# The low half of the rope keys for the second half of the queries: two products over 64 rows each, in opposite halves of TensorE's rows, in place of two products over 128 rows

## The chip, the cores and the metric

The kernel runs on one core of a Trainium2 chip. The metric is the device time of one execution in microseconds (us); a change is judged by the median of several executions.

## The reference

The reference is a decoder trunk of two layers over 256 tokens with a model width of 2048: a causal pooling layer, then a multi-head latent attention layer, each followed by a SwiGLU feed-forward part, and a final RMSNorm. What matters here is the score of each head:

```
sc = (jnp.einsum('bqhd,bkhd->bhqk', q_nope[:, s0:e], k_nope[:, :e])
      + jnp.einsum('bqhr,bkr->bhqk', q_pe[:, s0:e], k_pe[:, :e]))
sc = sc.astype(jnp.float32) * ATTN_SCALE
```

There are 16 heads. `q_nope` and `k_nope` have 128 features a head; `q_pe` has 64 rope features a head, and `k_pe`, also 64 features, is shared by all heads. The queries come in two blocks of 128: the first sees 128 keys, the second all 256. A masked softmax over the keys and the product with `v` follow.

## The kernel before, in words

Every operand of a product is split into a high and a low part, and a product is the sum high by high, high by low and low by high, each a matmul of its own into the same PSUM bank. ScalarE writes the high parts (of weights: `split`, L814) and VectorE subtracts to get the low parts (`split`, L1199). Weights arrive by DMA in chunks of up to 704 KB.

The attention works on pairs of heads, g = 0 to 7. TensorE runs nine slots in program order. Slot g (function `slot` in the TensorE block) makes queries, keys and values of pair g, and between these it does the attention of pair g - 1, so that the softmax of that pair (VectorE and ScalarE) lies beside matmuls of pair g. The order in a slot is: `query_rope_part` (12 matmuls), `scores` of the two heads hh = 0 and 1 of pair g - 1 (16 matmuls), `query_part` (24), `key_part` (24), `turn_probs` (six transposes), `value_part` (24), `head_output` (12). The last slot, g = 8, has parts of the output projection (`wo_part`) in place of the products of a pair.

`scores` writes head hh into bank SCORES + hh. Of the bank's 512 columns, columns 0 to 127 are the first query block against the first 128 keys and 384 to 511 hold the low part of that product; columns 128 to 383 are the second query block against all keys. The lines are L634, L635 and L636 for the first block, and for the second L640 to L642 (the 128 plain features) and L644 and L645 (the rope features). For the rope features `qpe_buf` holds the high part of a head's queries in one half of the 128 partitions and the low part in the other; head 1 has the halves the other way round. `kpe[:, 0]` holds the high keys in both halves, so L644 adds high by high and low by high in one matmul. `kpe[:, 1 + hh]` holds the low keys in the 64 partitions where head hh has its high queries, and zeros in the other 64. L645 multiplies all 128 rows with it: 64 rows count, 64 are multiplied by zero.

What follows the scores: the instruction of L645 raises `scores_ready`. VectorE (`row_max`, L1483 and on) waits for it, head 0 first; then come ScalarE's exponentials, VectorE's `rope_cos`, `normalise` (L1496, L1498), two splits of weights, `pair_lo` of queries and keys, `rope_lo`, and `probT_lo_half` (L1469), which raises `probT_split`. `head_output` (first matmul L671) of the same slot waits for it. In the same function, L598, L599 and L600 are `value_part`, L652 is `turn_probs`, L412 to L414 are the products of queries and keys.

The order of all queues is written out by hand; nothing else (no planner) orders the work.

Of the kernel before, what the change touches and what calls it, by code (L numbers as in the profile page):

```python
# [44 lines left out]
P = 128  # L45
SEQ = 256
# [4 lines left out]
NOPE, ROPE, V_DIM = 128, 64, 128  # L51
# [43 lines left out]
def chunk_plan():  # L95

    chunks, tiles, c, t = {}, {}, 0, 0
    for name, nc_, nt in (
        ("pool", 2 * GROUPS, DT),
        ("up0", 4 * FH, 2 * FH), ("down0", 2 * DT, DT), ("up1", 4 * FH, 2 * FH), ("down1", 2 * DT, DT),  # L100
        ("qa", 2 * LT, LT), ("kva", 2 * LT, LT), ("kpe", 2, 2),
        ("heads", 4 * HG, 8 * HG), ("wo", 2 * DT, DT),
        ("up2", 4 * FH, 2 * FH), ("down2", 2 * DT, DT), ("up3", 4 * FH, 2 * FH), ("down3", 2 * LAST_DT, LAST_DT), ("last", LAST_CHUNKS, 2),
    ):
        chunks[name], tiles[name] = c, t
        c, t = c + nc_, t + nt
    chunks["end"] = c
    return chunks, tiles


CHUNK, TILE = chunk_plan()
# [26 lines left out]
def plus(n, i, per):  # L138

    return n if i is None else i * per + n  # L140


def trunk(nc, xT, positions, consts, bands, gains, pool_w, w_kv_a, w_k_pe, w_q_a, w_kv_k, w_kv_v, w_q_nope, w_q_pe,
          w_o, w_gate, w_up, w_down, w_last, final_gain, out):
    with ExitStack() as ctx:
        def sem(name):
            return ctx.enter_context(nc.semaphore(name))
# [31 lines left out]
        def at(name, shape, dt, offset):  # L179
            return nc.alloc_sbuf_tensor_at(name, shape, dt, offset=offset)  # L180
# [21 lines left out]
        q_buf = at("q_buf", [P, 2, 2, 2 * SEQ], F32R, region_at + 8 * KB)  # L202
        v_buf = at("v_buf", [P, 2, 2, 2, 2 * V_DIM], F32R, region_at + 16 * KB)
        qpe_buf = at("qpe_buf", [P, 2, 2, SEQ], F32R, region_at + 24 * KB)
        kpe = at("kpe", [P, 3, SEQ], F32R, region_at + 28 * KB)
        heads = at("heads", [P, HG, 2, 2 * SEQ], F32R, region_at + 32 * KB)
# [24 lines left out]
        ps = ctx.enter_context(nc.psum_tensor("ps", [P, 8, 512], F32))  # L231

        SCORES, HEADS_OUT, STATS = 4, 6, 7
# [9 lines left out]
        evacuated = sem("evacuated")  # L243
# [38 lines left out]
        qpe_ready = sem("qpe_ready")  # L282
        kpe_ready = sem("kpe_ready")
# [6 lines left out]
        probT_split = sem("probT_split")  # L290
# [109 lines left out]
        def _(pe):  # L400
# [175 lines left out]
            def key_part(g, i=None):  # L576
                n, t = CHUNK["heads"] + 4 * g + 2, TILE["heads"] + 8 * g + 4
                pe.wait_ge(lo_ready, plus(made(n), i, BODY))
                for m in range(2):
                    bank_free(t + m, i, 16)  # L580
                    for kt in range(LT):
                        mm = product_one(n, m * LT + kt, (t + m) % 4, latent[:, KV, kt, :], kt == 0, kt == LT - 1)
                mm.then_inc(chunks_used, 1)
# [19 lines left out]
            def query_rope_part(g, i=None):  # L603
                n, t = CHUNK["heads"] + 4 * g, TILE["heads"] + 8 * g
                pe.wait_ge(lo_ready, plus(made(n), i, BODY))
                bank_free(t, i, 16)
                for kt in range(LT):
                    mm = product_one(n, kt, t % 4, latent[:, Q, kt, :], kt == 0, kt == LT - 1)
                mm.then_inc(chunks_used, 1)

            def query_part(g, i=None):
                n, t = CHUNK["heads"] + 4 * g + 1, TILE["heads"] + 8 * g + 2
                pe.wait_ge(lo_ready, plus(made(n), i, BODY))
                for m in range(2):
                    bank_free(t + m, i, 16)
                    for kt in range(LT):
                        mm = product_one(n, m * LT + kt, (t + m) % 4, latent[:, Q, kt, :], kt == 0, kt == LT - 1)
                mm.then_inc(chunks_used, 1)

            def scores(g, hh, i=None):  # L620

                b = g % 2
                if hh == 0:
                    pe.wait_ge(evacuated, plus(TILE["heads"] + 8 * g + 6, i, 16))
                    pe.wait_ge(qpe_ready, plus(g + 1, i, 2))
                    if g == 0:
                        pe.wait_ge(kpe_ready, 2)
                    if g >= 1:

                        pe.wait_ge(probT_split, plus(g, i, 2))  # L630
                bank = ps[:, SCORES + hh, :]
                first, k_both = slice(0, P), k_buf[:, b, hh, :].rearrange("p (o t) -> p o t", o=2)
                apart = bank.rearrange("p (c t) -> p c t", c=4)[:, 0:4:3, :]
                pe.matmul(apart, q_buf[:, b, hh, 0:P], k_both[:, :, 0:P], start=True, stop=False)  # L634
                pe.matmul(bank[:, first], q_buf[:, b, hh, SEQ:SEQ + P], k_buf[:, b, hh, 0:P], start=False, stop=False)  # L635
                pe.matmul(apart, qpe_buf[:, b, hh, 0:P], kpe[:, 0:2 + hh:1 + hh, 0:P], start=False, stop=True)  # L636
                dst, cols = bank[:, P:3 * P], slice(P, SEQ)
                q_hi, q_lo = q_buf[:, b, hh, cols], q_buf[:, b, hh, SEQ + P:]
                k_hi, k_lo = k_buf[:, b, hh, 0:SEQ], k_buf[:, b, hh, SEQ:]
                pe.matmul(dst, q_hi, k_hi, start=True, stop=False)  # L640
                pe.matmul(dst, q_hi, k_lo, start=False, stop=False)
                pe.matmul(dst, q_lo, k_hi, start=False, stop=False)  # L642
                both = qpe_buf[:, b, hh, cols]
                pe.matmul(dst, both, kpe[:, 0, :], start=False, stop=False)  # L644
                mm = pe.matmul(dst, both, kpe[:, 1 + hh, :], start=False, stop=True)  # L645
                mm.then_inc(scores_ready, 1)

            def turn_probs(g, hh, i=None):

                pe.wait_ge(prob_ready, plus(2 * (2 * g + hh + 1), i, 8))  # L650
                for c in range(3):
                    mm = pe.transpose(ps[:, SCORES + hh, c * P:(c + 1) * P], prob[:, hh, c * P:(c + 1) * P],  # L652
                                      const[:, C_IDENT:C_IDENT + P])
                mm.then_inc(probT_ready, 1)
# [21 lines left out]
            def wo_part(c, i=None, each=None):  # L676

                n, t = CHUNK["wo"] + c, TILE["wo"] + 4 * (c // BODY) + c % 4
                half = c // 4 % 2
                pe.wait_ge(lo_ready, plus(made(n), i, BODY))  # L680
                if half == 0:
                    bank_free(t, i, 4)
                for j in range(TILES):
                    kt = half * TILES + j
                    if each is not None:
                        each(kt)
                    mm = product3(n, j, t % 4, heads[:, kt // 2, kt % 2, :], kt == 0, kt == DT - 1)
                mm.then_inc(chunks_used, 1)

            def slot(g, i=None):  # L690


                own = g < HG
                if own:
                    query_rope_part(g, i)
                else:
                    wo_part(0)
                if g >= 1:
                    scores(g - 1, 0, i)
                    scores(g - 1, 1, i)  # L700
                if own:
                    query_part(g, i)
                    if g == 0:
                        pe.wait_ge(lat_ready, 2 * LT)
                    key_part(g, i)
                else:
                    wo_part(1)
                    wo_part(2)
                if g >= 1:
                    turn_probs(g - 1, 0, i)  # L710
                    turn_probs(g - 1, 1, i)
                if own:
                    value_part(g, i)
                else:
                    wo_part(3)
                if g >= 1:
                    head_output(g - 1, 0, i)
                    head_output(g - 1, 1, i)

            pe.wait_ge(lat_ready, LT)  # L720
            slot(0)
            slot(1)

            with pe.Fori(0, HG // 2 - 1) as i:
                slot(2, i)
                slot(3, i)
# [52 lines left out]
            both = LAST_CHUNKS - SPLIT_SLOTS  # L779
# [7 lines left out]
            for c in range(both, LAST_CHUNKS):  # L787
                pe.wait_ge(lo_ready, made(CHUNK["last"] + c))
                mm = last_part(c, 0)
# [1000 lines left out]
```

## Time and profile before

| | |
|---|---|
| median of 3 runs | 1781.75 us (1781.26 to 1782.9) |
| the profiled execution | 1783.35 us, its span 1781.4 us |
| TensorE (matmuls), busy | 1766.1 us, 99% of the span |
| TensorE weight loads, busy | 1562.5 us, 88% |
| TensorE's share of the chain that ended last | 97% |
| VectorE, ScalarE, GpSimd, busy | 64%, 51%, 6% |
| mean granted TensorE clock | 0.999 |
| attention slots g = 1 to 8 in the span | about 846 to 960 us |

The span is the time from the first to the last instruction; the execution's own time is a little longer. A row of the matmul engine shows how long one matmul was in the pipeline, which overlaps with the next; what a matmul costs in a stream is the distance from its start to the next start. "PEld" is the loading of a matmul's stationary operand, one for each matmul, which runs beside the matmul before.

### The profile page before, as it was taken

To read this page: it belongs to the slowest core of one execution; us is meant where nothing else is said; L and a number is where in the kernel's file an instruction comes from. 1 tells how busy PE (TensorE), PEld (TensorE's weight loads), DVE (VectorE), ACT (ScalarE), POOL (GpSimd) and SP (SyncE) were. 2 spreads that over 40 slices of the span, in tenths; PEclk is the share of its full clock that TensorE was granted. 3 is DMA by queue.
4 is the path that set the end of the run, shared out by engine and by line. 5 is a ranking of instruction groups with operands and counts; after the bars stand their busy time and mean duration, and the time that the engine had idled before them with its cause. 6 is when DMAs were issued, how large, how long until landed. Compare 5 with 4: busy or idle time off the path is not lost.

```text
span 1781.4 us, 29177 instructions
## 1 busy us (share of the span) xinstructions
PE 1766.1 (99%) x10376; PEld 1562.5 (88%) x10376; DVE 1137.8 (64%) x1456; ACT 915.5 (51%) x1176; POOL 113.2 (6%) x129
## 2 busy tenths in 40 slices
PE   9999999999999999999999999999999999999998
PEld 5888888888888888888999888888888888888886
DVE  4866666556666666668997776666655566666553
ACT  5766664334444444455775456666533344445433
POOL 2200000000000001123112420000000000000000
PEclk9999999999999999999999999999999999999999
DMA  6555557545555566544444555555665455556641
GB/s 250 198 190 189 190 189 238 193 158 173 188 188 188 188 224 199 174 152 138 142 154 154 189 189 188 189 188 188 221 204 177 156 189 188 190 190 223 225 147 71
DMA packets 85008, 328.26 MB, mean 184 GB/s; under 512 B 9568, under 2 KB 10336, under 8 KB 84832
## 3 DMA queue, kind: packets, MB, share of 16 engines
q1 hardware_dynamic: 84816, 326.57, 54.6%
q10 hardware_dynamic: 144, 1.05, 0.1%
q8 instruction: 30, 0.49, 0.1%
q14 instruction: 18, 0.15, 0.0%
HBM read 325.48 MB, written 2.10 MB: 184 GB/s over the span
## 4 chain that ended last, share of the span: by engine, by line
PE 97%; DVE 2%; ACT 0%; DMA 0%; issue 0%; POOL 0%; SPq 0%; ACTq 0%; POOLq 0%; DVEq 0%
PE ps L404 57%; PE ps L405 30%; PE ps L475 2%; PE ps L412 1%; PE ps L413 1%; PE ps L414 1%; PE ps L765 1%; PE ps L763 1%; PE ps L764 1%; DMA raw<-pool_w 0%; DVE w_lo L1199 0%; PE ps L598 0%; PE ps L599 0%; PE ps L600 0%; POOL square_sum L1672 0%
## 5 line engine op out<-in xcount | busy, mean ns | idle before, releaser
L1199 DVE TENSOR_TENSOR w_lo<-raw,w_hi 128x1024 fp32r<-128x1024 f32 (+2 forms) x564 | 737.5, 1309 | 421.0 <-ACT w_hi L814 418.7
L404 PE MATMUL ps<-xg,w_hi 128*128 128x512 f32 x2880 | 999.5, 390 | 0.5 <-issue 0.5
L814 ACT ACTIVATE w_hi<-raw 128x1024 fp32r<-128x1024 f32 (+2 forms) x565 | 632.0, 1120 | 552.5 <-PE ps L405 538.2
L405 PE MATMUL ps<-xg,w_lo 128*128 128x256 f32 x2880 | 812.1, 282 | 0.0
L404 PEld LDWEIGHTS ps<-xg,w_hi 128*128 128x128 f32 x2880 | 540.4, 188 | 113.8 <-issue 0.6
L405 PEld LDWEIGHTS ps<-xg,w_lo 128*128 128x128 f32 x2880 | 544.3, 189 | 0.1
L404 PE MATMUL ps<-act,w_hi 128*128 128x512 f32 x1320 | 458.0, 390 | 0.0
L405 PE MATMUL ps<-act,w_lo 128*128 128x256 f32 x1320 | 372.2, 282 | 0.0
L404 PEld LDWEIGHTS ps<-act,w_hi 128*128 128x128 f32 x1320 | 247.7, 188 | 51.9
L405 PEld LDWEIGHTS ps<-act,w_lo 128*128 128x128 f32 x1320 | 249.5, 189 | 0.0
L1279 DVE TENSOR_TENSOR sums<-ps,cross 128x512 f32<-128x512 f32 x88 | 60.9, 692 | 95.5 <-ACT cross L891 95.5
L891 ACT ACTIVATE cross<-ps 128x512 f32<-128x512 f32 x88 | 52.6, 598 | 120.6 <-PE ps L405 120.5
L404 PE MATMUL ps<-heads,w_hi 128*128 128x512 f32 x256 | 89.1, 391 | 0.0
L1630 POOL TENSOR_TENSOR square<-x 128x256 f32 (+1 forms) x32 | 33.2, 1039 | 765.2 <-DVE x L1300 765.2
L405 PE MATMUL ps<-heads,w_lo 128*128 128x256 f32 x256 | 72.2, 282 | 0.0
L1299 DVE TENSOR_TENSOR x<-ps,x 128x256 f32 (+1 forms) x76 | 32.1, 422 | 54.9 <-PE ps L405 54.9
L1283 DVE TENSOR_TENSOR sums<-sums,rstd 128x512 f32<-128x512 f32 x88 | 60.9, 692 | 3.0
L894 ACT ACTIVATE gate_act<-sums 128x256 f32<-128x256 f32 x88 | 36.8, 418 | 46.0 <-DVE sums L1283 45.8
L826 ACT ACTIVATE xg<-x,gain 128x256 fp32r<-128x256 f32 (+1 forms) x48 | 23.4, 508 | 66.5 <-DVE x L1300 62.1
L404 PEld LDWEIGHTS ps<-heads,w_hi 128*128 128x128 f32 x256 | 48.1, 188 | 9.9
L405 PEld LDWEIGHTS ps<-heads,w_lo 128*128 128x128 f32 x256 | 48.4, 189 | 0.0
L412 PE MATMUL ps<-latent,w_hi 128*128 128x256 f32 x160 | 45.2, 283 | 2.5 <-DVE gate_act L1456 2.3
(196 smaller groups left out, 1227.7 us busy)
## 6 DMA issues: line engine op xcount, KB each, us to landing
raw<-w_gate SPq DMA_DIRECT2D x176, 512.0 KB, 3.2
raw<-w_up SPq DMA_DIRECT2D x176, 512.0 KB, 3.2
raw<-w_down SPq DMA_DIRECT2D x120, 704.0 KB, 4.1
raw<-w_o SPq DMA_DIRECT2D x32, 512.0 KB, 3.2
raw<-w_last SPq DMA_DIRECT2D x11, 512.0 KB, 3.2
raw<-pool_w SPq DMA_DIRECT2D x8, 512.0 KB, 12.0
raw<-w_q_a SPq DMA_DIRECT2D x8, 512.0 KB, 3.3
raw<-w_kv_a SPq DMA_DIRECT2D x8, 512.0 KB, 3.2
```

Source lines behind the costliest of these rows:

```text
L404: pe.matmul(ps[:, bank, :], w_hi[:, s, j * P:(j + 1) * P], moving, start=start, stop=False)
L405: return pe.matmul(ps[:, bank, 0:SEQ], w_lo[:, s, j * P:(j + 1) * P], moving[:, 0:SEQ], start=False, stop=stop)
L412: pe.matmul(dst, w_hi[:, s, j * P:(j + 1) * P], moving[:, 0:SEQ], start=start, stop=False)
L475: mm = pe.matmul(ps[:, 4 + 2 * (g % 2) + s, :], x_pool[:, GT * g + kt, s * P:(s + 1) * P], raw[:, c, j * GT * P:(j + 1) * GT * P], start=( ...
L814: nc.scalar.activation(dst, src, ACT.Copy).then_inc(hi_ready, 1)
L891: nc.scalar.activation(cross[:, :, :], ps[:, bank:bank + 2, SEQ:], ACT.Copy).then_inc(cross_ready, 1)
L894: nc.scalar.activation(gate_act[:, :], sums[:, 0, :], ACT.Silu).then_inc(gate_ready, 1)
L1199: nc.vector.tensor_tensor(lo, src, hi.bitcast(F32), ALU.subtract).then_inc(lo_ready, 1)
L1279: nc.vector.tensor_tensor(sums[:, :, :], ps[:, bank:bank + 2, 0:SEQ], cross[:, :, :], ALU.add).then_inc(evacuated, 2)
L1283: nc.vector.tensor_tensor(sums[:, :, :], sums[:, :, :], r, ALU.mult).then_inc(sums_ready, 1)
L1299: step(nc.vector.tensor_tensor(xd, ps[:, b, 0:SEQ], xd, ALU.add))
L1630: step(nc.gpsimd.tensor_tensor(square[:, :], src, src, ALU.mult))
```

## The change

A new function `rope_low` issues the two matmuls of L645, of both heads, ahead of `scores`. Each is restricted to the 64 partitions that count: head 0 has partitions 0 to 63, head 1 has 64 to 127, and they go to banks SCORES and SCORES + 1. They now open the accumulation of their bank (`start=True`), and L634 and L640 no longer do. The waits that stood at the head of `scores` move into `rope_low`, in the same place of the stream. `scores` then has seven matmuls a head, and the one of L644 raises `scores_ready`. The number of matmuls stays at 16 a pair of heads.

```diff
+            def rope_low(g, i=None):
+                b = g % 2
+                pe.wait_ge(evacuated, plus(TILE["heads"] + 8 * g + 6, i, 16))
+                pe.wait_ge(qpe_ready, plus(g + 1, i, 2))
+                if g == 0:
+                    pe.wait_ge(kpe_ready, 2)
+                if g >= 1:
+                    pe.wait_ge(probT_split, plus(g, i, 2))
+                for hh in range(2):
+                    rows = slice(ROPE * hh, ROPE * hh + ROPE)
+                    pe.matmul(ps[:, SCORES + hh, P:3 * P], qpe_buf[rows, b, hh, P:SEQ], kpe[rows, 1 + hh, :],
+                              start=True, stop=False)
...
             def scores(g, hh, i=None):
                 b = g % 2
-                if hh == 0:
-                    pe.wait_ge(evacuated, plus(TILE["heads"] + 8 * g + 6, i, 16))
-                    pe.wait_ge(qpe_ready, plus(g + 1, i, 2))
-                    if g == 0:
-                        pe.wait_ge(kpe_ready, 2)
-                    if g >= 1:
-                        pe.wait_ge(probT_split, plus(g, i, 2))
...
-                pe.matmul(apart, q_buf[:, b, hh, 0:P], k_both[:, :, 0:P], start=True, stop=False)
+                pe.matmul(apart, q_buf[:, b, hh, 0:P], k_both[:, :, 0:P], start=False, stop=False)
...
-                pe.matmul(dst, q_hi, k_hi, start=True, stop=False)
+                pe.matmul(dst, q_hi, k_hi, start=False, stop=False)
...
-                both = qpe_buf[:, b, hh, cols]
-                pe.matmul(dst, both, kpe[:, 0, :], start=False, stop=False)
-                mm = pe.matmul(dst, both, kpe[:, 1 + hh, :], start=False, stop=True)
+                mm = pe.matmul(dst, qpe_buf[:, b, hh, cols], kpe[:, 0, :], start=False, stop=True)
                 mm.then_inc(scores_ready, 1)
...
                 if g >= 1:
+                    rope_low(g - 1, i)
                     scores(g - 1, 0, i)
                     scores(g - 1, 1, i)
```

## Rows read from the trace of the kernel before

**Rows 1.** The page: busy us, share of the span and instructions of each engine.

```profile
PE 1766.1 (99%) x10376; PEld 1562.5 (88%) x10376; DVE 1137.8 (64%) x1456; ACT 915.5 (51%) x1176; POOL 113.2 (6%) x129
```

**Rows 2.** Busy time by window, slot 3: window, length, PE, PEld, DVE, ACT, POOL.

```profile
873.90:887.80 13.90, 13.90 (x119) 13.90 (x120) 12.97 (x33) 10.34 (x22) 1.60 (x2) 1.00 0.43 135
```

**Rows 3.** Waits between 859 and 943.3: us in total, times, longest.

```profile
DVE prob L1483 <- PE ps L645: 2.8, 6, 0.7
...
PE ps L671 <- DVE probT L1469: 0.4, 1, 0.4
```

**Rows 4.** Timeline of slots 2, 3 and 7: VectorE's chain and TensorE's start on `head_output`.

```profile
863.73 0.29 DVE L1483 TENSOR_TENSOR prob<-ps,const 128x128 f32<-128x128 f32 x1 [0.67 <-PE ps L645]
...
872.85 0.95 DVE L1469 TENSOR_TENSOR probT<-ps,probT 128x768 fp32r<-128x768 f32 x1
...
873.46 0.28 PE L600 MATMUL ps<-w_hi,latent 128*128 128x256 f32 x1
873.90 0.36 PE L671 MATMUL ps<-probT,v_buf 128*128 128x256 f32 x1 [0.17 <-issue]
...
886.63 0.95 DVE L1469 TENSOR_TENSOR probT<-ps,probT 128x768 fp32r<-128x768 f32 x1
...
887.63 0.28 PE L600 MATMUL ps<-w_hi,latent 128*128 128x256 f32 x1
887.75 0.29 PE L671 MATMUL ps<-probT,v_buf 128*128 128x256 f32 x1
...
942.53 0.95 DVE L1469 TENSOR_TENSOR probT<-ps,probT 128x768 fp32r<-128x768 f32 x1
...
942.95 0.27 PE L600 MATMUL ps<-w_hi,latent 128*128 128x256 f32 x1
943.58 0.36 PE L671 MATMUL ps<-probT,v_buf 128*128 128x256 f32 x1 [0.35 <-issue]
```

**Rows 5.** Timeline of TensorE in slot 3, head 0 of the scores.

```profile
876.75 0.28 PE L634 MATMUL ps<-k_buf,q_buf 128*128 128x256 f32 x1
...
876.93 0.33 PE L636 MATMUL ps<-kpe,qpe_buf 128*128 128x256 f32 x1
877.10 0.28 PE L640 MATMUL ps<-k_buf,q_buf 128*128 128x256 f32 x1
...
877.58 0.28 PE L645 MATMUL ps<-kpe,qpe_buf 128*128 128x256 f32 x1
877.70 0.28 PE L634 MATMUL ps<-k_buf,q_buf 128*128 128x256 f32 x1
```

**Rows 6.** Timeline of TensorE in `head_output` of slot 2: two matmuls of 128 columns.

```profile
874.39 0.28 PE L672 MATMUL ps<-probT,v_buf 128*128 128x128 f32 x1
874.50 0.27 PE L673 MATMUL ps<-probT,v_buf 128*128 128x128 f32 x1
```

**Rows 7.** Line L645: duration ns least/median/most, first and last start.

```profile
L645 PEld LDWEIGHTS ps<-kpe,qpe_buf x16: 187/188/192, 847.5 to 949.5; 128*128 128x128 f32 x16
```

**Rows 8.** Timeline of TensorE in slot 2, into and out of the six transposes.

```profile
869.96 0.28 PE L414 MATMUL ps<-latent,w_lo 128*128 128x256 f32 x1
870.08 0.82 PE L652 MATMUL ps<-const,prob 128*128 128x128 f32 x6
870.65 0.36 PE L598 MATMUL ps<-w_hi,latent 128*128 128x256 f32 x1
870.85 0.28 PE L599 MATMUL ps<-w_lo,latent 128*128 128x256 f32 x1
```

**Rows 9.** Timeline of slots 1 and 8, where VectorE comes to the scores late.

```profile
849.08 0.35 PE L412 MATMUL ps<-latent,w_hi 128*128 128x256 f32 x1 [0.24 <-DVE v_buf L1447]
...
852.84 0.36 PE L412 MATMUL ps<-latent,w_hi 128*128 128x256 f32 x1 [0.71 <-DVE gate_act L1456]
...
950.30 0.29 DVE L1483 TENSOR_TENSOR prob<-ps,const 128x128 f32<-128x128 f32 x1
...
958.78 0.36 PE L671 MATMUL ps<-probT,v_buf 128*128 128x256 f32 x1
```

More of the change, by code:

```diff
@@ L633, in scores @@
                 apart = bank.rearrange("p (c t) -> p c t", c=4)[:, 0:4:3, :]
-                pe.matmul(apart, q_buf[:, b, hh, 0:P], k_both[:, :, 0:P], start=True, stop=False)
+                pe.matmul(apart, q_buf[:, b, hh, 0:P], k_both[:, :, 0:P], start=False, stop=False)
                 pe.matmul(bank[:, first], q_buf[:, b, hh, SEQ:SEQ + P], k_buf[:, b, hh, 0:P], start=False, stop=False)
-                pe.matmul(apart, qpe_buf[:, b, hh, 0:P], kpe[:, 0:2 + hh:1 + hh, 0:P], start=False, stop=True)
+                pe.matmul(apart, qpe_buf[:, b, hh, 0:P], kpe[:, 0:2 + hh:1 + hh, 0:P], start=False, stop=False)
                 dst, cols = bank[:, P:3 * P], slice(P, SEQ)
```

## Prediction

> **What bounds the kernel now.** I read the page first: TensorE is busy in 1766.1 of 1781.4 us and VectorE in 64% [rows 1]. So the end is set by TensorE's stream, and a change in it is worth what it does to the distances between starts. But the change sits in the attention, a stage of its own, so next come the busy times by window. In slot 3, 13.9 us long, VectorE is busy 12.97 us, 93% and not 64% [rows 2]: two engines are nearly equal here. The waits of that stage say how they are tied. VectorE waits for L645, the end of the scores, six times (2.8 us in all), and TensorE waits at `head_output` (L671) for VectorE's L1469 [rows 3].
>
> The timeline makes this exact. In slot 2 VectorE starts on the scores at 863.73 and ends L1469 at 872.85 + 0.95 = 873.80: 10.07 us in which it hardly ever rests. TensorE's last matmul of `value_part` starts at 873.46, a stream goes on after 0.118 (873.58), yet L671 starts at 873.90, 0.10 after L1469's end [rows 4]. TensorE lost 0.32 us. In slot 7 the same sum gives 943.58 - (942.95 + 0.118) = 0.51 us lost. In slot 3 L1469 ends at 887.58, L671 could have started at 887.68 and started in stride at 887.75: nothing lost, 0.07 to spare [rows 4]. These three stand for six slots (2 to 7); by the same sum slot 4 loses 0.07, and slots 5 and 6 have 0.05 and 0.13 to spare. So in slots 2 to 7 there is a loop: scores of head 0, VectorE's chain of 9.6 to 10.3 us, `head_output`, the next slot's rope queries, scores again. It bounds slots 2, 4 and 7 and misses the others by a tenth of a us. What counts is then two numbers: **d1**, how much later the scores of head 0 come (this delays the loop), and **d2**, how much longer TensorE's stream gets a slot. A slot pays d2 or, if VectorE's chain is last, d1 less what it had to spare.
>
> Slots 1 and 8 are different. In slot 8 VectorE comes to the scores only at 950.30, long after L645; in slot 1 TensorE waits right behind the scores 0.24 and then 0.71 us for VectorE's evacuations [rows 9]. Small shifts of the scores are swallowed there; in slot 8 L671 too stands 0.11 us behind its stride, waiting for L1469 (by the sum above, with the L405 before it at 958.55).
>
> **The change part by part.** No other engine's instruction, no DMA and no queue but TensorE's is touched. The four waits move with the first matmul and stay at the same place of the stream; before, none of them held it (L634 at 876.75 follows in stride), so they cost nothing. Which matmul carries `start` changes no instruction and no count; I take it at nothing.
>
> *The matmuls.* A matmul of 256 columns in this stream costs 0.118 us (877.58 to 877.70 [rows 5]). The change removes L645 from each head (-2 x 0.118 = -0.236 a slot) and adds a pair ahead, at a price p. Head 0 loses one matmul of its own and has the pair in front: d1 = p - 0.118. The stream: d2 = p - 0.236. All hangs on p, and no row of the trace has a matmul over 64 rows. Bounds without a cost for changing over: 0.118 if the two run fully side by side, 0.236 if one behind the other.
>
> Which is nearer? In `head_output` a matmul of 128 columns costs 0.11 (874.39 to 874.50 [rows 6]), almost what 256 columns cost; and L634, L635, L636 together stream 640 columns in 0.35 (876.75 to 877.10 [rows 5]), three strides. The number of columns doesn't set the stride: each matmul brings a load of its weights (188 ns a row of its own, overlapping [rows 7]), and loads follow each other no faster than about one in 0.11. The pair has two loads and the matmul behind it a third. Matmuls that run side by side gain nothing if their loads still come one by one. I take p = 0.236 for the pair itself.
>
> The Trainium skill says the same of the load: in "TensorE: Matmul & The Clock Gate", section "LDWEIGHTS (loading the stationary operand)", its time goes by the columns, not by the rows of the contraction. No row here has a load of 64 rows. The same page, in "Part 3: Packing small matmuls — row/col tiling", has matmuls in different row groups run together with starts 4 ns apart; that is the first rival below.
>
> *The change-over.* The array goes from 128 rows to 64 and back, eight times. The trace has no such step. Its nearest is the passage through the transposes, another manner of using the array: into them 0.12 us (869.96 to 870.08), which is the stride, and out of them 0.20 in place of 0.118 (870.65 to 870.85) [rows 8], so 0.08 for the round trip. The lower bound is nothing. For the upper one the array would empty and load again at each of the two changes: L645's matmul is in the pipe for 0.28 and costs 0.118, so emptying shows 0.16, and a load that nothing hides 0.19 [rows 5, 7], 0.35 in all, 0.70 a slot. I take the nearest row, 0.08 a slot.
>
> "TensorEngine Tiling (Array Packing)" in the Trainium skill, section "Tiling Modes", says that a change of tiling mode, not merely of tile, drains TensorE. The transposes don't test this, and it speaks against the change; it is the second rival.
>
> *The sum.* p = 0.236 + 0.08 = 0.316, d1 = +0.20, d2 = +0.08. Slots 2, 4 and 7 pay d1: 0.60. Slot 3 pays 0.20 - 0.07 = 0.13, slot 5 0.15, slot 6 0.08 (both sums give that, d1 less 0.13 or d2): 0.36. Slots 1 and 8 swallow 0.08. Together +0.96, say +1.0 us. The profiled execution, 1783.35 us (its span and 1.95 around it), would become 1784.3. It lies 1.6 above the median of the runs; from the median 1781.75 the forecast is **1782.7 us**, a change of +0.06%. A difference under 0.2% (3.6 us) is about what a measurement of this kernel can't tell from no change, so this is "same".
>
> **The rivals.**
>
> *Side by side, and nothing for the change-over.* p = 0.118, so d1 = 0 and d2 = -0.118. It needs weight loads that overlap, or are shorter for 64 rows. Even then the loop takes most of it: slots 2, 4 and 7 don't move (VectorE's chain starts when it did), slot 3 gains 0.07, slot 5 0.05, slot 6 0.118, slots 1 and 8 nothing. That is -0.24 us: 1781.5 us. In other words, the most that the title promises, 8 x 0.118 = 0.94 us, is out of reach by three quarters. For it: nothing in the trace excludes it. Against: rows 5 and 6. Chance 0.22.
>
> *The array empties twice a slot and loads bare.* p = 0.236 + 0.70 = 0.94, d1 = 0.82, d2 = 0.70. Slots 2, 4 and 7: 2.46. Slots 3, 5 and 6: 0.75 + 0.77 + 0.70 = 2.22. Slot 8: 0.70 - 0.11 = 0.59. Slot 1's own waits (0.95 together) swallow it. Together +5.3 us: 1787.0 us, +0.30%, slower. It comes out as slower from a cost of about 0.25 us a change-over, since then 8 slots near 0.5 us reach 3.6. If only emptying shows (0.16 each, weights loaded ahead), p = 0.56, d1 = 0.44, d2 = 0.32: 1.32 + 0.37 + 0.39 + 0.32 + 0.21 = +2.6 us, 1784.4, not yet slower. For it: a stationary operand over other rows may not be loadable behind a running matmul of 128 rows. Against: the transposes pass without it. Chance 0.22 for the whole and what lies between it and the half.
>
> *The halves don't pack and the loop shifts otherwise.* VectorE's chain varies from 9.6 to 10.3 us between slots that do the same work; another phase of its splits against GpSimd and ScalarE could move each slot by some tenths to either side, up to 2 us in all. Chance 0.04.
>
> **How the numbers follow.** The forecast has 0.52: change-over costs from nothing (slots 2, 4, 7 pay 0.118, in all +0.5) to 0.33 a slot (+2.6 us). Low end: the first rival, 1781.5, less 0.6 for spread of the median of few runs. High end: near the second rival, 1786.6. Slower by over 0.2% needs 1785.3: most of the second rival, 0.18. Faster by over 0.2% has no mechanism, since even the removed 0.94 us is 0.05%: 0.02. Same: 0.80.
>
> **What the changed profile would show.** The two matmuls of `rope_low` with 64 rows: starts a few ns apart would mean the first rival, 0.11 apart the forecast. The distance from the first of them to head 0's L634 is p; over 0.5 means that the array emptied. The last L414 before them and the first start show the way in. L671's lag behind the stride in slots 2, 4 and 7 should grow by d1 - d2 = 0.12 whatever the change-over costs. VectorE's wait before L1483 should grow a little. I am wrong if p is under 0.2 or over 0.5, if the slots' sum differs from +1.0 us by more than p explains, or if a stage outside 846 to 960 us moves.

## The result, and the profile after

| | before | changed |
|---|---|---|
| median | 1781.43 us (22 runs) | 1783.99 us (22 runs) |
| ratio to before, 95% interval | | 1.0014 [1.0008, 1.0019] |
| profiled execution, its span | 1783.35, 1781.4 us | 1783.71, 1781.8 us |

The change costs 2.56 us, 0.14%. The interval, some 1.4 to 3.4 us, leaves out zero, so the cost is real; it is below the 0.2% taken in the prediction as the bound of "same". The forecast of 1782.7 us had the sign, and 40% of the size (+1.0 forecast from 1781.75). The page of the changed kernel hardly shows anything:

```profile
PE 1767.7 (99%) x10376; PEld 1562.2 (88%) x10376; DVE 1137.5 (64%) x1456; ACT 916.0 (51%) x1176; POOL 113.2 (6%) x129
```

The two profiled spans differ by only 0.4 us, because the execution of before that was profiled had lost about 2 us before the attention: its last L414 ahead of slot 1's scores starts at 846.68, that of the changed kernel at 844.53. So all readings below are distances within the attention. I use three, each from the start of the last matmul ahead of the scores (L414; in slot 8 it is an L405 of the output projection): the **way**, to head 0's first matmul of the second query block (L640; L647 in the changed kernel, whose lines lie 5 to 7 lower on TensorE); **hh0**, to head 0's last matmul, which releases VectorE (L645; L650 in the changed kernel); and the **pass**, to the last matmul of head 1. The start of slot 3's scores before:

```profile
876.64 0.27 PE L414 MATMUL ps<-latent,w_lo 128*128 128x256 f32 x1
```

Here is slot 3 of the changed kernel, matmuls (columns as in [rows 5]):

```profile
874.90 0.27 PE L414 MATMUL ps<-latent,w_lo 128*128 128x256 f32 x1
875.10 0.38 PE L632 MATMUL ps<-kpe,qpe_buf 64*128 64x256 f32 x2
875.41 0.39 PE L641 MATMUL ps<-k_buf,q_buf 128*128 128x256 f32 x1
875.64 0.22 PE L642 MATMUL ps<-k_buf,q_buf 128*128 128x128 f32 x1
875.70 0.33 PE L643 MATMUL ps<-kpe,qpe_buf 128*128 128x256 f32 x1
875.87 0.28 PE L647 MATMUL ps<-k_buf,q_buf 128*128 128x256 f32 x1
...
876.23 0.28 PE L650 MATMUL ps<-kpe,qpe_buf 128*128 128x256 f32 x1
...
877.06 0.28 PE L650 MATMUL ps<-kpe,qpe_buf 128*128 128x256 f32 x1
```

and the weight loads of the same stretch:

```profile
874.78 0.19 PEld L414 LDWEIGHTS ps<-latent,w_lo 128*128 128x128 f32 x1
875.10 0.19 PEld L632 LDWEIGHTS ps<-kpe,qpe_buf 64*128 64x128 f32 x2
875.41 0.19 PEld L641 LDWEIGHTS ps<-k_buf,q_buf 128*128 128x128 f32 x1
875.52 0.19 PEld L642 LDWEIGHTS ps<-k_buf,q_buf 128*128 128x128 f32 x1
```

Two things are to be seen. First, the pair is a pair. Two matmuls (x2) take 0.38 together, and the view of line L632 gives 0.38 for each single one, so both run over the same time. Their two weight loads, 0.19 together, coincide as well:

```profile
L632 PEld LDWEIGHTS ps<-kpe,qpe_buf x16: 182/183/183, 844.7 to 948.0; 64*128 64x128 f32 x16
L632 PE MATMUL ps<-kpe,qpe_buf x16: 379/380/383, 844.7 to 948.0; 64*128 64x256 f32 x16
```

Second, neither the step to 64 rows nor the step back is free. In a stream the load of the next matmul starts one stride ahead of it (874.78 for the L414 at 874.90). L632's load starts only at 875.10, and so does its matmul's row; L641's load starts with L641's own row at 875.41. No load is hidden at either change. The rows of these matmuls are 0.1 longer (0.38, 0.39 against 0.28), which I read as the wait for the bare load, the one that nothing hides. From L414 to L647 the way is 0.97 us; before it was 877.10 less 876.64, 0.46. So p = 0.97 - 0.46 = **0.51 us**, hh0 grew from 0.94 to 1.33 (d1 = 0.39) and the pass from between 1.88 and 1.89 to between 2.15 and 2.16 (d2 = 0.27), in each of the eight slots within 0.02.

How that turns into time is to be read at `head_output`, in slots 2 and 7 (the lines L1475, L600 and L676 answer to L1469, L600 and L671 of [rows 4]):

```profile
871.11 0.95 DVE L1475 TENSOR_TENSOR probT<-ps,probT 128x768 fp32r<-128x768 f32 x1
...
871.59 0.28 PE L600 MATMUL ps<-w_hi,latent 128*128 128x256 f32 x1
872.16 0.35 PE L676 MATMUL ps<-probT,v_buf 128*128 128x256 f32 x1 [0.29 <-issue]
...
942.93 0.28 PE L600 MATMUL ps<-w_hi,latent 128*128 128x256 f32 x1
943.69 0.35 PE L676 MATMUL ps<-probT,v_buf 128*128 128x256 f32 x1 [0.48 <-issue]
```

The distance from L600 to the first matmul of `head_output` was 0.44 in slot 2 and 0.63 in slot 7, and is 0.57 and 0.76 now: 0.13 more each, which is d1 - d2 = 0.12. In slot 4 it went from 0.19 to 0.31. VectorE's chain itself, from the start on the scores to the end of L1475, is as long as before in slots 2 to 7, within 0.02 us (10.08 and 10.27 us in slots 2 and 7, against 10.07 and 10.27), so the rival by which that chain shifts of itself is out. The wait of VectorE for the scores grew too:

```profile
DVE prob L1489 <- PE ps L650: 5.5, 6, 1.1
```

It was 2.8 us in six waits [rows 3]. From the last matmul ahead of slot 1's scores to that ahead of slot 8's there were 101.00 us before (846.68 to 947.68) and 103.27 now (844.53 to 947.80): +2.27. In slot 8 the distance from that matmul to `head_output` grew from 11.10 to 11.37. Together +2.54 us. Behind it, from the first matmul of `head_output` in slot 8 to the end of the span, both have 822.6 us. So the distances place the whole cost in the attention. That they come so close to the 2.56 between the medians is in part chance, since the medians are not known to 0.02 us.

### The profile page after: what moved, and what is told of

It reads as the page before. It is cut to its first block, busy times and chain, and to the rows that moved or that the text cites. A ratio compares the mean times of both kernels' runs of the same rounds, so it can differ in the third digit from the quotient of the medians.

```text
span 1781.8 us, 29177 instructions
## 1 busy us (share of the span) xinstructions
PE 1767.7 (99%) x10376; PEld 1562.2 (88%) x10376; DVE 1137.5 (64%) x1456; ACT 916.0 (51%) x1176; POOL 113.2 (6%) x129
## 4 chain that ended last, share of the span: by engine, by line
PE 97%; DVE 2%; ACT 0%; POOL 0%; issue 0%; ACTq 0%; POOLq 0%; DVEq 0%
PE ps L404 57%; PE ps L405 30%; PE ps L475 2%; PE ps L412 1%; PE ps L414 1%; PE ps L413 1%; PE ps L771 1%; PE ps L769 1%; PE ps L770 1%; DVE w_lo L1205 0%; PE ps L599 0%; PE ps L598 0%; PE ps L600 0%; POOL square_sum L1678 0%; PE ps L676 0%
## 5 line engine op out<-in xcount | busy, mean ns | idle before, releaser
L404 PE MATMUL ps<-xg,w_hi 128*128 128x512 f32 x2880 | 999.5, 390 | 0.5 <-issue 0.5
L405 PE MATMUL ps<-xg,w_lo 128*128 128x256 f32 x2880 | 812.1, 282 | 0.0
L404 PEld LDWEIGHTS ps<-xg,w_hi 128*128 128x128 f32 x2880 | 540.6, 188 | 113.8 <-issue 0.6
L405 PEld LDWEIGHTS ps<-xg,w_lo 128*128 128x128 f32 x2880 | 544.3, 189 | 0.1
L404 PE MATMUL ps<-act,w_hi 128*128 128x512 f32 x1320 | 458.1, 390 | 0.0
L405 PE MATMUL ps<-act,w_lo 128*128 128x256 f32 x1320 | 372.2, 282 | 0.0
L404 PEld LDWEIGHTS ps<-act,w_hi 128*128 128x128 f32 x1320 | 247.8, 188 | 51.9
L405 PEld LDWEIGHTS ps<-act,w_lo 128*128 128x128 f32 x1320 | 249.5, 189 | 0.0
L404 PE MATMUL ps<-heads,w_hi 128*128 128x512 f32 x256 | 89.1, 391 | 0.0
L405 PE MATMUL ps<-heads,w_lo 128*128 128x256 f32 x256 | 72.2, 282 | 0.0
L404 PEld LDWEIGHTS ps<-heads,w_hi 128*128 128x128 f32 x256 | 48.1, 188 | 10.0
L405 PEld LDWEIGHTS ps<-heads,w_lo 128*128 128x128 f32 x256 | 48.4, 189 | 0.0
```

The source lines that it names most:

```text
L404: pe.matmul(ps[:, bank, :], w_hi[:, s, j * P:(j + 1) * P], moving, start=start, stop=False)
L405: return pe.matmul(ps[:, bank, 0:SEQ], w_lo[:, s, j * P:(j + 1) * P], moving[:, 0:SEQ], start=False, stop=stop)
```

## The experiments

The theory after the result was: each change of the array between 128 and 64 rows costs about 0.195 us, the pair itself one stride of 0.118; and the later scores of head 0 delay a loop through VectorE. All times are medians beside runs of the kernel before on the same chip. In the edits, lines are those of the changed kernel unless the kernel before is named.

**Order and start flags alone.**

```diff
-                    rows = slice(ROPE * hh, ROPE * hh + ROPE)
+                    rows = slice(0, P)
```

> The changed kernel, but the two matmuls moved ahead run over all 128 rows (zeros included) as they did before the change; order, start flags and waits are those of the changed kernel. Measured by two distances: 'way' is from the last L414 before the scores to head 0's first matmul of the second block (0.46 us before, 0.97 changed), 'pass' from that L414 to the last matmul of head 1 (1.885 before, 2.16 changed). Theory (each change of the array between 128 and 64 rows costs about 0.195 us, the pair itself one stride of 0.118): way 0.46 + 0.118 = 0.58, pass 1.885; only head 0's scores come 0.118 later, time +0.5 us over before. Rival (the new order or the start flags cost it): way stays at 0.97, time stays at +2.5 us.

Measured: 1782.27 us against 1781.7, ratio 1.0003 [0.9993, 1.0012]. hh0 is 1.06, pass 1.88. In slot 3:

```profile
876.55 0.28 PE L414 MATMUL ps<-latent,w_lo 128*128 128x256 f32 x1
876.67 0.40 PE L632 MATMUL ps<-kpe,qpe_buf 128*128 128x256 f32 x2
876.90 0.28 PE L641 MATMUL ps<-k_buf,q_buf 128*128 128x256 f32 x1
```

The stream runs on in stride, 0.12 and then 0.23 for two matmuls. The way is 0.70 and not 0.58: I had counted one of the two matmuls that are now ahead. The two distances that carry the verdict came as the theory has them: pass unchanged, hh0 0.12 later. The +0.57 us between the medians is within their uncertainty; by distances it is +0.64 from slot 1 to slot 8 and +0.02 in slot 8. So the order and the flags explain about a quarter of the 2.54 us (through the loop), the 64 rows the rest.

**What a pair costs without its changes of rows.**

```diff
-                for hh in range(2):
+                for k, hh in enumerate((0, 1) * 4):
                     rows = slice(ROPE * hh, ROPE * hh + ROPE)
                     pe.matmul(ps[:, SCORES + hh, P:3 * P], qpe_buf[rows, b, hh, P:SEQ], kpe[rows, 1 + hh, :],
-                              start=True, stop=False)
+                              start=True, stop=(k < 6))
```

> The changed kernel with the pair of 64-row matmuls issued four times in a row (each overwrites the one before, the scores stay the same). Theory: the change-over is paid twice a slot as before, each further pair costs only itself. If its loads overlap like its matmuls, 0.118 a pair: way 0.97 + 0.35 = 1.32. If the loads come one by one, 0.22 a pair: way 1.63. Rival (64-row matmuls are slow in themselves and no change-over exists): 0.39 + 0.118 = 0.51 a pair, way 2.5. Time over the changed kernel: 8 x 0.35 = +2.8 us, 8 x 0.66 = +5.3 us, or 8 x 1.5 = +12 us.

Measured: 1786.6 us against 1781.7, ratio 1.0027 [1.0017, 1.0037]: 4.9 us over before where the changed kernel is 2.56 over, so 2.3 more and not the 2.8 expected; slot 1 swallows its share again (15.81 us long, 15.80 in both kernels). Way 1.32 to 1.33, the theory's 1.32. In slot 3, matmuls:

```profile
877.06 0.28 PE L414 MATMUL ps<-latent,w_lo 128*128 128x256 f32 x1
877.27 0.74 PE L632 MATMUL ps<-kpe,qpe_buf 64*128 64x256 f32 x8
877.94 0.38 PE L641 MATMUL ps<-k_buf,q_buf 128*128 128x256 f32 x1
...
878.16 0.22 PE L642 MATMUL ps<-k_buf,q_buf 128*128 128x128 f32 x1
```

Eight matmuls over 64 rows take 0.74 where two take 0.38: 0.12 for each further pair. So a pair, matmuls and loads, costs the stride of a single matmul of 128 rows.

The same rows suggest how the cost divides between the way in and the way out. This rests on the ends of the matmul rows, which the profile models; a run measures only the sum. A row without a bare load is 0.28 long, so the last pair streams from 877.27 + 0.74 - 0.28 = 877.73, the first pair three strides earlier at 877.38. From L414 at 877.06 that is 0.32, 0.20 over a stride. L642 at 878.16 is in stride, so L641 streams from 878.04: 0.31 after the last pair, 0.19 over. By this reading both changes cost alike.

**Is it the opposite halves?**

```diff
-                    rows = slice(ROPE * hh, ROPE * hh + ROPE)
+                    rows = slice(0, ROPE)
```

> The changed kernel with both heads' 64-row products on partitions 0 to 63 (for head 1 these are the wrong rows, so its scores leave that product out). Theory (the pair runs side by side because its halves differ): the second must now follow the first, +0.118 if its load hides, up to +0.19 if not: way 1.09 to 1.16, pass 2.28 to 2.35, time +0.9 to +1.5 us over the changed kernel. Rival (nothing runs side by side, the pair costs two strides): way stays at 0.97, time as the changed kernel.

Measured: 1784.91 us against 1781.7, ratio 1.0018 [1.0008, 1.0028]: 3.2 us over before, 0.65 more than the changed kernel, where 0.9 to 1.5 was expected. The time alone would not tell the two apart, the distances do (104.04 us from slot 1 to slot 8, against 103.27). Way 1.09, pass 2.27. The two matmuls and their neighbours:

```profile
875.62 0.28 PE L414 MATMUL ps<-latent,w_lo 128*128 128x256 f32 x1
875.83 0.50 PE L632 MATMUL ps<-kpe,qpe_buf 64*128 64x256 f32 x2
876.26 0.38 PE L641 MATMUL ps<-k_buf,q_buf 128*128 128x256 f32 x1
```

0.50 in place of 0.38: they follow each other by a stride. The opposite halves are what puts them side by side, and between matmuls over the same 64 rows the load hides.

**The pair taken apart.**

```diff
-                    rope_low(g - 1, i)
+                    rope_low(g - 1, 0, i)
                     scores(g - 1, 0, i)
+                    rope_low(g - 1, 1, i)
                     scores(g - 1, 1, i)
```

`rope_low` here issues the matmul of one head; the waits stay ahead of head 0's.

> The changed kernel with the pair taken apart: head 0's 64-row matmul ahead of head 0's scores, head 1's ahead of head 1's. Four changes of rows a slot in place of two, and no pair. Theory (0.195 a change, a single one costs 0.118 + 0.39 = 0.51): way 0.97 as changed, pass 1.885 - 0.236 + 2 x 0.51 = 2.67. Time: TensorE's stream +0.78 a slot over before, less what its waits swallow, about +5 to +6 us over before. Rival (the cost belongs to the 64-row matmuls, 0.25 each, not to the change of rows): way 0.72, pass 2.16, time as the changed kernel or less.

Measured: 1786.49 us against 1781.7, ratio 1.0028 [1.0017, 1.004]. Way 0.97, pass 2.66. That is 4.8 us over before, a little under the 5 to 6 expected; TensorE's own waits at `head_output` took more of it (its first matmul is now in stride in slots 2 to 6), and slot 1 swallowed its share (15.82 us). Head 1's single matmul, ahead of its scores:

```profile
876.84 0.28 PE L650 MATMUL ps<-kpe,qpe_buf 128*128 128x256 f32 x1
877.05 0.38 PE L632 MATMUL ps<-kpe,qpe_buf 64*128 64x256 f32 x1
877.36 0.39 PE L641 MATMUL ps<-k_buf,q_buf 128*128 128x256 f32 x1
877.58 0.23 PE L642 MATMUL ps<-k_buf,q_buf 128*128 128x128 f32 x1
```

One matmul costs the same 0.51 as the pair did, and a second passage costs as much again. The cost belongs to the change of rows and not to the matmuls.

**Four pairs against eight matmuls of 128 rows.** The edit of the four pairs, with `rows = slice(0, P)`.

> As the run with four pairs, but all eight matmuls run over 128 rows: no change of rows and nothing side by side. Each overwrites the one before it, the scores stay the same. Theory: eight strides of 0.12, way 0.46 + 0.96 = 1.42, against 1.325 with the four pairs. So at four pairs a passage the packing wins 0.09 us a slot, though it loses 0.27 with one pair; time 0.7 us below the four pairs' time plus 0.7, that is 1786.6 + 8 x 0.09 = 1787.3 us. Rival (side by side brings nothing, the four pairs are only cheap because 64 rows are): way equal to or under 1.325.

Measured: 1787.07 us against 1781.31, ratio 1.0033 [1.0021, 1.0045]. Way 1.42 as expected, against 1.32 for the four pairs. In slot 3:

```profile
875.41 0.27 PE L414 MATMUL ps<-latent,w_lo 128*128 128x256 f32 x1
875.52 1.11 PE L632 MATMUL ps<-kpe,qpe_buf 128*128 128x256 f32 x8
876.47 0.28 PE L641 MATMUL ps<-k_buf,q_buf 128*128 128x256 f32 x1
```

Over before it is 5.8 us against 4.9 for the four pairs, which these few runs hardly tell apart; but the distances differ by this 0.1 in all eight slots. The packing itself works; with four pairs of 256 columns in one passage it has just paid for its two changes. Three pairs were not run; by the numbers above they would cost 0.39 + 3 x 0.118 = 0.74 against 0.71, a small loss.

**What the change could at most have taken.** The kernel before, without L645:

```diff
-                pe.matmul(dst, both, kpe[:, 0, :], start=False, stop=False)
-                mm = pe.matmul(dst, both, kpe[:, 1 + hh, :], start=False, stop=True)
+                mm = pe.matmul(dst, both, kpe[:, 0, :], start=False, stop=True)
```

> The kernel before without L645: high queries by low rope keys are left out for the second block of queries. This is what the change could at most have taken away, both strides. Theory (a loop of VectorE's chain and TensorE bounds slots 2, 4 and 7): head 0's scores come 0.118 earlier and the stream is 0.236 a slot shorter, so slots 2, 4 and 7 gain only 0.118, slot 3 0.19, slot 5 0.17, slot 6 0.236, slots 1 and 8 nothing or little: -0.95 us (to -1.2 with slot 8). Rival (TensorE's stream alone bounds): 8 x 0.236 = -1.9 us.

Measured: 1780.54 us against 1781.6, -1.06 us, ratio 0.9992 [0.9983, 1.0001]. The interval doesn't settle it alone; the distances do. hh0 is 0.82, pass 1.65, so the stream lost 0.235 a slot, but from slot 1 to slot 8 there are 100.29 us against 101.00, and 0.23 less in slot 8: -0.94. So half of the 1.9 us is swallowed, 0.24 by slot 1's own waits (15.81 us long) and 0.70 by the loop in slots 2 to 7. That the sum meets the -0.95 expected is luck: that sum gave slot 8 nothing, and it gave slots 3, 5 and 6 0.60 where they gained 0.42. Even leaving the whole product out would bring no more than 0.06%.

**The loop opened, on both kernels.** On VectorE, in `slot`:

```diff
-                    pair_lo(g, 2, k_buf, i)
                     probT_lo_half(g - 1, i)
+                    pair_lo(g, 2, k_buf, i)
```

On the kernel before:

> The kernel before with one swap on VectorE: probT_lo_half (L1469) ahead of pair_lo of the keys, so TensorE's head_output is released 0.6 to 0.7 us earlier. Theory (the loop): L671 follows in stride in slots 2 to 8; they give back 0.32 + 0.07 + 0.51 + 0.11 = 1.0 us, slot 1 up to 0.5 more: -1.0 to -1.5 us, 1780.2. Rival (TensorE waits there for something else, or waits later for the keys instead): no change within 0.3 us, with a new wait on k_buf's line.

Measured: 1779.51 us against 1781.6, ratio 0.9987 [0.9978, 0.9996]: 2.1 us under the kernel before, where 1.0 to 1.5 were expected. Slot 2:

```profile
871.57 0.96 DVE L1469 TENSOR_TENSOR probT<-ps,probT 128x768 fp32r<-128x768 f32 x1
872.45 0.68 DVE L1441 TENSOR_TENSOR k_buf<-ps,k_buf 128x512 fp32r<-128x512 f32 x1
```

```profile
872.80 0.28 PE L600 MATMUL ps<-w_hi,latent 128*128 128x256 f32 x1
872.91 0.28 PE L671 MATMUL ps<-probT,v_buf 128*128 128x256 f32 x1
```

L1469 ends at 872.53, TensorE comes at 872.91 and doesn't wait: 0.11 after L600, in stride, in all of slots 1 to 7. Nor does it wait for the keys instead, as the rival had it: slots 2 to 6 are 13.78 or 13.79 us long, as slots 3 and 6 were before. From slot 1 to slot 8 there are 99.32 us, 1.68 less. 0.32 + 0.07 + 0.51 are the waits of slots 2, 4 and 7, 0.52 that of slot 1 (its distance went from 0.64 to 0.12). The other 0.26 is what I had left out: after each wait the next matmul follows L671 by 0.19 or 0.20 and not by 0.12, since its load too has fallen behind, so four waits less are worth some 0.25 more. Slot 8 gave nothing, though 0.11 was expected: it has no keys to swap with, and `head_output` stays 11.10 us behind. The last 0.4 up to the medians is within their uncertainty.

On the changed kernel:

> The changed kernel with the same swap on VectorE. Theory: the loop no longer bounds, so what is left of the change is TensorE's own stream, 0.27 a slot: the kernel before with the swap + 8 x 0.27 = +2.2 us; against the changed kernel -1.4 to -2.0 us (its lags at head_output in slots 2 to 8 were 0.45 + 0.05 + 0.19 + 0.06 + 0 + 0.64 + 0.09). Rival (the change costs by delaying VectorE alone): the swap makes it equal to the kernel before with the swap.

Measured: 1781.84 us against 1781.6, ratio 0.9999 [0.999, 1.0008]. That is 2.2 us under the changed kernel, more than the 1.4 to 2.0 expected, which had left out the late load as well. It is 2.3 over the kernel before with the same swap, where 8 x d2 = 2.2 was expected. By distances it is less: slots 2 to 6 are 14.03 or 14.04 us long, against 13.78 or 13.79, 0.25 more each; slot 7 has 0.37 more, slot 8 0.27, and slot 1 swallows its share (15.19 against 15.22), 1.87 in all. The 0.4 between this and the medians is within their uncertainty. So with the loop opened nearly all that is left of the change is TensorE's longer stream, and it is still a loss; the rival, no difference, is out by the distances.

## Why the prediction was right, and where it was not

- *What bounds the stage* held: two engines tied in a loop, with slots 2, 4 and 7 bound by VectorE's chain. The swap on VectorE shows it, and the lag at `head_output` grew in slots 2, 4 and 7 by the 0.12 that was forecast whatever the change-over costs.
- *The working from p to the time* held. With the measured d1 = 0.39 and d2 = 0.27 the prediction's own sum gives 3 x 0.39 for slots 2, 4 and 7 and 0.32 + 0.34 + 0.27 for slots 3, 5 and 6, 2.10 us; measured were 2.27. The difference sits in slots 3, 5 and 6 (0.38, 0.38 and 0.31 from their L414 to the next one), where TensorE now waits or nearly waits and pays the late load behind a wait: the second matmul of `head_output` follows the first by 0.19 or 0.20 there, against 0.11 to 0.14 before. Slot 1 swallowed its share (15.80 us before and after). Slot 8 did not, though I had said it would: VectorE's chain there grew with TensorE's stream (8.38 to 8.66 us), so the lag of about 0.1 us stayed and the slot paid the whole 0.27. The link is ScalarE, whose split of a weight waits for an L405 of TensorE, and VectorE's next split waits for ScalarE. Before, and changed:

```profile
955.50 1.06 ACT L814 ACTIVATE w_hi<-raw 128x1024 fp32r<-128x1024 f32 x1 [1.29 <-PE ps L405]
955.89 1.06 ACT L820 ACTIVATE w_hi<-raw 128x1024 fp32r<-128x1024 f32 x1 [1.58 <-PE ps L405]
```

- *The price of the pair* was wrong, too high: 0.236, measured 0.118. The step was "matmuls that run side by side gain nothing if their loads still come one by one". Loads for opposite halves run together. The reading behind that step, that the number of columns doesn't set the stride, holds from 128 to 256 columns only [rows 6]: in slot 8 of the kernel before, a matmul of 512 columns takes 0.22, from the start of L404 to that of L405 (the two rows below). That a load's pace is what holds the shorter ones at 0.11 stays argued. The load's length was right: 183 ns for 64 rows against 188 for 128 [rows 7], as the Trainium skill has it in "TensorE: Matmul & The Clock Gate", section "LDWEIGHTS (loading the stationary operand)"; and that matmuls in different row groups run together is what "Part 3: Packing small matmuls — row/col tiling" of the same page states; here the two rows coincide to within 0.01 us (0.38 together, 0.38 each).

```profile
947.46 0.39 PE L404 MATMUL ps<-heads,w_hi 128*128 128x512 f32 x1
947.68 0.28 PE L405 MATMUL ps<-heads,w_lo 128*128 128x256 f32 x1
```

- *The change-over* was the term that was mis-sized: taken at 0.08 a slot after the transposes [rows 8], measured 0.51 - 0.118 = 0.39. That row was the wrong neighbour: transposes of all 128 rows make no change of rows. The rule of the Trainium skill in "TensorEngine Tiling (Array Packing)", section "Tiling Modes", that a change of tiling mode drains TensorE, agrees with the trace: two changes a slot lengthen the way by 0.39 over the stride of a pair, and four (the pair taken apart) cost twice that. It was a rival with 0.22. The bound that I set for it, 0.35 a change, was too high against 0.195. The trace shows no load hidden, and read off the rows the load costs 0.1 rather than its row's 0.19, and the emptying 0.08 to 0.09 rather than 0.16 (875.10 against the stride's 875.02, and rows of 0.38 against 0.28); no experiment separated the two.
- The two errors stand against each other, -0.12 and +0.31 on p, and that they partly cancel is luck. With the pair priced rightly and the change-over as I took it, the forecast would have been p = 0.20, d1 = 0.08 and d2 = -0.04, about +0.24 us, a tenth of what was measured. By the test that the prediction set itself, p over 0.5, it was just outside. The range held by its upper bounds and not by its middle. Nearest came a number inside the second rival, 1784.4 us with p = 0.56 if only the emptying shows; its mechanism is not what happened either, since the loads are not hidden and the pair is cheaper.
- *Order and flags* were rightly taken at nothing for TensorE's stream: with 128 rows in the new order the pass is 1.88.

## What to carry to other kernels

Matmuls over 64 rows in opposite halves run as one, loads included, but entering and leaving such a passage cost 0.39 us together here, more than three strides of 256 columns: with matmuls of this size pack four pairs or more in one passage, or none. Other numbers of columns were not run. Before pricing an edit by strides, see whether the engine that issues it waits for another further down the same slot; if so, what counts is when the other engine is released, and the cheapest gain may be a swap in that engine's queue (here 2.1 us by the medians and 1.7 by the distances, from one call moved up, where leaving out the whole product was worth 1.06 and 0.94).

## What the runs showed of the hardware

- Weight loads of two matmuls over opposite 64-row halves start together, and a pair costs one stride: three further pairs add 0.355 us to one pair's way, 0.118 each.
- Between 64-row matmuls over the same half the next load hides as between full ones (0.118 from one to the next); in the scores it is hidden everywhere except where the number of rows changes. A change from 128 to 64 rows and back costs 0.39 us, with one matmul between or with four pairs.
- Kernels that do the same work up to the attention reached its slot 1 between 844.5 and 846.7 us in ten profiled executions. For the two compared above the difference arises in the first 50 us, in which TensorE had 180 matmuls in the one of before and 194 in the changed one; what causes it is not shown, and it is not tied to the change (the two edited kernels without it reach slot 1 at 844.84 and 846.58). A profiled span alone can't rank kernels that differ by 2 us.
